# The first two gate tiles of each merge, loaded during the stage in front of it

## The reference

```
# first block, 3 branches of width 512          # second block, 5 branches of width 256
proj  = einsum('bsgc,gcd->bsgd', branches, w_branch[l])
gates = sigmoid(gate_logits.reshape(B, S, N_BRANCH, D_MODEL))     # gate_logits: columns of norm(x) @ w_in
x = x + sum(gates * proj, axis=2) @ w_out[l]
```

## Time and profile before

| | |
|---|---|
| median of three runs | 3766.71 us (3765.52, 3766.71, 5822.26) |
| profiled execution, its time | 3761.98 us |
| its span | 3760.2 us |
| mean granted TensorE clock | 0.961 |
| TensorE matmuls busy | 3514.6 us, 93% of the span |
| VectorE, ScalarE busy | 51%, 38% |
| HBM read, written | 307.09 MB, 38.80 MB |
| merges begin (first load issued) | 519.35, 1607.88, 2765.47, 3544.43 us |

### The profile page before, as it was taken

The page is one execution under the profiler, slowest core; times in us unless marked ns, Lnnn a source line. Parts: engine busy times, 40 slices in busy tenths (PEclk is TensorE's granted clock), DMA queues, the critical chain, the costliest instruction groups (busy, mean ns, idle before and its releaser), DMA issues. The chain is left out here.

```text
span 3760.2 us, 53758 instructions
## 1 busy us (share of the span) xinstructions
PE 3514.6 (93%) x21928; PEld 2747.8 (73%) x21928; DVE 1900.7 (51%) x3211; ACT 1419.0 (38%) x2319; POOL 61.4 (2%) x44
## 2 busy tenths in 40 slices
PE   8899789999999898989999999999989999899898
PEld 6678568788877786678788877756668778566586
DVE  6633433577557433434577353137655542367454
ACT  6222332344335221433344223255543333545532
POOL 0011000000000100000000000000000000000000
PEclk9999989999999998999999999999999999999999
DMA  4211323222332213142223233212133332122242
GB/s 151 67 59 33 139 107 109 79 99 97 107 124 76 60 55 112 48 146 101 84 95 107 83 125 112 91 41 87 49 132 134 111 110 85 37 90 65 99 140 76
DMA packets 101477, 350.04 MB, mean 93 GB/s; under 512 B 10945, under 2 KB 11329, under 8 KB 98433
## 3 DMA queue, kind: packets, MB, share of 16 engines
q1 hardware_dynamic: 101248, 346.85, 26.7%
HBM read 307.09 MB, written 38.80 MB: 92 GB/s over the span
## 5 line engine op out<-in xcount | busy, mean ns | idle before, releaser
L213 PE MATMUL bank<-h_high,weights_high 128*128 128x512 f32 x2464 | 1007.6, 409 | 69.6 <-DVE weights_low L1528 40.3
L214 PE MATMUL bank<-h_low,weights_high 128*128 128x512 f32 x2464 | 976.4, 396 | 0.0
L215 PE MATMUL bank<-h_high,weights_low 128*128 128x512 f32 x2464 | 975.3, 396 | 0.0
L213 PEld LDWEIGHTS bank<-h_high,weights_high 128*128 128x128 f32 x2464 | 471.6, 191 | 188.9 <-DVE weights_low L1528 42.8
L215 PEld LDWEIGHTS bank<-h_high,weights_low 128*128 128x128 f32 x2464 | 470.7, 191 | 104.0
L214 PEld LDWEIGHTS bank<-h_low,weights_high 128*128 128x128 f32 x2464 | 472.4, 192 | 100.4 <-issue 5.7
L1482 ACT CAST weights_high<-ring 128x1024 fp32r<-128x1024 f32 (+1 forms) x128 | 144.9, 1132 | 520.9 <-PE bank L215 467.5
L1528 DVE TENSOR_TENSOR weights_low<-ring,weights_high 128x1024 fp32r<-128x1024 f32 (+1 forms) x128 | 169.5, 1324 | 333.4 <-ACT weights_high L1482 333.2
L206 DVE TENSOR_TENSOR weights_low<-ring,weights_high 128x1024 fp32r<-128x1024 f32 x140 | 171.1, 1222 | 329.4 <-ACT weights_high L201 327.4
L201 ACT CAST weights_high<-ring 128x1024 fp32r<-128x1024 f32 x140 | 146.4, 1046 | 464.9 <-PE bank L215 458.0
L1655 ACT CAST weights_high<-ring 128x1024 fp32r<-128x1024 f32 (+1 forms) x116 | 132.6, 1143 | 337.9 <-PE bank L215 337.9
(11 more groups left out here) (431 smaller groups left out, 5252.2 us busy)
## 6 DMA issues: line engine op xcount, KB each, us to landing
ring<-in_in SPq DMA_DIRECT2D x136, 512.0 KB, 3.6
ring<-in_up SPq DMA_DIRECT2D x88, 512.0 KB, 3.2
x<-in_gates SPq DMA_DIRECT2D x64, 512.0 KB, 3.9
ring<-in_gates SPq DMA_DIRECT2D x64, 512.0 KB, 3.3
ring<-in_down SPq DMA_DIRECT2D x32, 704.0 KB, 4.1
ring<-in_out SPq DMA_DIRECT2D x32, 512.0 KB, 3.2
ring<-in_branch SPq DMA_DIRECT2D x16, 768.0 KB, 4.4
stored<-g_spill SPq DMA_DIRECT2D x16, 768.0 KB, 4.6
```

The lines of the kernel that those rows point to most:

```text
L213: pe.matmul(bank, core.wh[:, half, w], high, start=start, stop=False)
L214: pe.matmul(bank, core.wh[:, half, w], low, start=False, stop=False)
L215: return pe.matmul(bank, core.wl[:, half, w], high, start=False, stop=stop)
```

## The change

Every merge gets its tiles 0 and 1 from the stage in front of it. SP issues the two loads at the end of its program there, `branches` after the wait for the landed spills and a wait for the eight `y_mm` steps (the last readers of `scores` and `qdec`), `attention` after the wait for the spills alone. They go to the slots that the merge would use, columns 0 to 1023 and 1536 to 2559 in the first block, 0 to 1023 and 1280 to 2303 in the second. To keep those columns free, `vt` changes places with `scores` and `qdec`, `probsT` goes from columns 0 to 2047 to 3072 to 5119, and the two staging tiles go to 0 to 1023. A third set of four semaphores, made once, counts the landings; `merge` takes it as its `landed` and clears it at its end as it did its own. Sizes, number and order of the loads are the same, and so is all arithmetic.

```diff
+def load_merge(sp, core, n, slot_w, width, src):
+
+    sp.dma_start(core.ring[:, n * slot_w:n * slot_w + width], src).then_inc(core.landed[2][n], 16)
+
...
-def branches(nc, core, b, y_rw, y, y_sg, e):
+def branches(nc, core, b, y_rw, y, y_sg, e, first_gates):
...
             extra_transfers(sp, sems, core, e, begun=True)
+            sp.wait_ge(sems["y_mm"], 2 * NCH)
+            for n in range(2):
+                load_merge(sp, core, n, 12 * P, KD * P, first_gates(n))
...
                   "taken", "added", "y_rounded", "y_split", "m_rounded", "m_split", "projected", "x_added", *ROOT) as (block, sems):
+                  "taken", "added", "y_rounded", "y_split", "m_rounded", "m_split", "projected", "x_added", *ROOT,
+                  landed=core.landed[2]) as (block, sems):
...
-            for n in range(RING):
+            for n in range(2, RING):
                 load(n)
...
-            b["vt"] = core.ring[:, 0:4 * T].rearrange("p (c n) -> p c n", c=NCH)
-            b["scores"] = core.ring[:, 4 * T:8 * T].rearrange("p (c n) -> p c n", c=NCH)
-            b["qdec"] = core.ring[:, 8 * T:10 * T].rearrange("p (m t) -> p m t", m=2)
+            b["scores"] = core.ring[:, 0:4 * T].rearrange("p (c n) -> p c n", c=NCH)
+            b["qdec"] = core.ring[:, 4 * T:6 * T].rearrange("p (m t) -> p m t", m=2)
+            b["vt"] = core.ring[:, 6 * T:10 * T].rearrange("p (c n) -> p c n", c=NCH)
...
         @block.sync
         def _(sp):
             extra_transfers(sp, sems, core, e)
+            for n in range(2):
+                load_merge(sp, core, n, 2 * N_BR2 * P, KD * P, first_gates(n))
...
-                b["probsT"] = core.ring[:, 0:4 * T].rearrange("p (a h t) -> p a h t", a=2, h=2)
+                b["probsT"] = core.ring[:, 6 * T:10 * T].rearrange("p (a h t) -> p a h t", a=2, h=2)
...
-                    core.banks[7:8], [core.ring[:, n * T:(n + 1) * T] for n in (8, 9)]))
+                    core.banks[7:8], [core.ring[:, n * T:(n + 1) * T] for n in range(2)]), gates)
```

More of the change, by code:

```diff
@@ L1403, in merge @@
             phase(nc, *LANDED, "stored0", "stored1", "reloaded", "loaded", "gate_mm", "branch_mm", "rounded", "split", "gated", "opened",
-                  "taken", "added", "y_rounded", "y_split", "m_rounded", "m_split", "projected", "x_added", *ROOT) as (block, sems):
+                  "taken", "added", "y_rounded", "y_split", "m_rounded", "m_split", "projected", "x_added", *ROOT,
+                  landed=core.landed[2]) as (block, sems):
         def width(n):
@@ L1829, in block1_layer @@
                      *((("y", c), 4) for c in range(NCH)), ("sums", 8), ("turned", 8)],
-                    core.banks[6:7], [staging[:, n, :] for n in range(2)]))
+                    core.banks[6:7], [staging[:, n, :] for n in range(2)]), lambda n: w["gates1"][layer * (3 * KD) + n])
                 core.slots = core.ring
@@ L1835, in units @@
             return lambda n: w[name][layer * count + n]
-        one, other = core.landed
+        one, other = core.landed[0:2]
         with split_weights(nc, core, 12), nc.sbuf_tensor(f"y_high1{layer}", [P, 12, T], F32R) as y_high, \
@@ L2493, in _, with attention @@
                 beside(n)
-def attention(nc, core, b, pairs, forgotten, e):
+def attention(nc, core, b, pairs, forgotten, e, first_gates):
     banks, ident = core.banks, core.ident2
@@ L3075, in program @@
         core.count = 0
-        core.landed = [[stack.enter_context(nc.semaphore(f"{side}_{name}")) for name in LANDED] for side in ("one", "other")]
+        core.landed = [[stack.enter_context(nc.semaphore(f"{side}_{name}")) for name in LANDED] for side in ("one", "other", "third")]
         core.root, core.ones, core.eps, core.tiny = (buf(stack, "root", [T]), buf(stack, "ones", [P]), buf(stack, "eps", [2]),
```

## The result

The changed kernel takes 3746.7 us in the median of four runs (3745.53 to 3748.11). Of four runs of before one took 5822.26 us and is left out as a slow one; the others took 3765.52, 3766.71 and 3771.58 us. The ratio to them is 0.9943, with a 95% interval of 0.9929 to 0.9958. The forecast was 3751.8 us and 0.9960.

What follows compares the result with a forecast made beforehand. TensorE has work nearly throughout; its idle stretches at merge starts include waits for tile 0's load. Removing these gives 14.9 us, all else 0: 3766.7 - 14.9 = 3751.8 us; forecast 3744 to 3758, 8-of-10 range 3742 to 3761.

Steps and rivals of the forecast that it cites:

- The wait for tile 0: At each merge's start, SP's issue to ScalarE's cast: 15.29 us over four merges less 0.4, gain 14.9 (14.1 to 15.3).
- The wait for tile 1: At a merge's start, tile 1's load is covered by TensorE's work on tile 0: gain 0.
- SP's longer program, tenants, clearing: Two more loads in the stage in front, moved buffers, and four semaphores cleared at a merge's end: cost 0 each.
- The queue at a merge's start: Later loads issue 0.8 us earlier but are needed 3.3 to 4.9 us earlier; merge 3's stored gates are tight: cost 0.
- the guard of 2 us: In merge 3, TensorE keeps 2 us of room even if the stored gates come no earlier.
- Rival B: Gain given back within the merge by x's reload or the stored gates; if half were lost, 3759 us; chance 6%.
- The clock: Slow stretch after each merge's restart costs 1.4 to 2.9 us, left as is; scatter some +-3 us over four merges.
- rival A: Clock stays up after the shorter pause at each merge's start: some 8 us more gain, 3744 us; chance 8%.
- The range: Forecast case for the whole kernel: 3744 to 3758 us, at 77%.

Runs made afterwards that it cites:

- the tenants' run: Tenants change places and the third semaphore set is used, but all four first tiles load in the merge; against the kernel before: 3766.98 us, ratio 1.0000.
- tile 0 alone: The change with only tile 0 loaded ahead and tile 1 loaded first in the merge, against the kernel before: 3753.11 us, ratio 0.9962.
- The experiment with four loads more: Whole change plus four unread 512 KB loads behind the two ahead, awaited at the end of the stage in front; against the kernel before: 3750.75 us, ratio 0.9967.
- the first block's gain: Only the first block's two merges get tiles ahead, against the kernel before: 3757.34 us, ratio 0.9974.
- the halves: Whole change with tile 0's cast and subtraction in two halves of 512 columns, against the kernel before: 3747.60 us, ratio 0.9954.
- the fastest version: Whole change, tile 0's cast and subtraction in halves, and semaphore clearing shared by five engines, against the kernel before: 3718.37 us, ratio 0.9877.
- the second: The unaltered changed kernel timed in more rounds on one chip, against the kernel before: 3750.02 us, ratio 0.9955.
- the traffic added: Whole change plus four unread 512 KB loads, in all stages in front or in attention alone, against the kernel before: ratios 0.9967 and 0.9962.
- sharing the clearing: The kernel before with each stage's semaphores cleared by all five engines in turns instead of SP alone: 3742.20 us, ratio 0.9940.

## Why the prediction was right

*The wait for tile 0.* Read from the distance between SP's issue and ScalarE's cast, it was 15.29 us less 0.1 us per merge. ScalarE in fact starts 0.02, 0.02, 0.03 and 0.01 us after SP's first issue (the entries are 517.84, 1599.13, 2755.40 and 3533.13), so the term was 15.2, nearer its upper bound of 15.3 than the 14.9 forecast. TensorE's idle time fell by 4.75 us in merge 1 and 2.97 in merge 4, the sum of its waits by 15.0. Tenants and tile 0 alone show that nothing else carries the gain.

*The wait for tile 1.* Priced at nothing, and shown to within what can be measured: without that load ahead TensorE waits 0.4 us more in sum, and the time's interval includes the whole change's.

*SP's longer program, tenants, clearing.* Priced at nothing, and shown by the tenants' run and by SP's loads at 506.27, landing within 4.5 us. The experiment with four loads more shows what the cover is: there is room in `branches` for the two that the change lays there, and not for six when the stage has to wait for their landing.

*The queue at a merge's start.* The tight place was the stored gates of merge 3. They come 12.4 us after their issue at 2756.72, at 2769.1, and their sigmoid starts at 2769.55, right behind the gate's; the guard of 2 us wasn't needed. Rival B is out by the stage lengths and by the additivity of the first block's gain.

*The clock.* I gave it +-3 us. After the restart the granted clock stays at 0.50 for 4.7, 5.4, 6.2 and 3.3 us in the four merges; before it was 5.7, 3.8, 3.8 and 3.0, and in the changed kernel's second profile 4.5, 4.9, 3.5 and 3.1. That is scatter and no trend, and rival A (the clock stays up after a shorter pause) didn't happen in any of the four.

The reason that I gave against rival A was misread, though. The 0.69 ahead of merge 3 is a mean over a window in which the clock fell and rose again. Cut into pieces (us, TensorE's busy time and matmuls, granted clock, DMA share, GB/s), the kernel before shows the end of TensorE's work, the start of its pause, and the rest of the pause with the restart:

```profile
2761.30:2762.60 1.30, 1.27 (x24) 1.00 0.00 0
2762.60:2764.60 2.00, 0.00 (x0) 1.00 0.00 0
2764.70:2774.80 10.10, 3.71 (x9) 0.50 0.86 332
```

The clock is up when the pause begins and falls 2 us into it. In merges 2 and 4 of before it was also still at 1.00 some 4 us into the pause, and only ahead of merge 1 had it fallen with TensorE at work. So in three merges of four the low clock of the restart came with the pause and was not there before it, and a shorter pause may bear on it. Two cases speak for that. With the halves, merge 3 restarts after 4.3 us at 1.00, and the clock falls only 1.1 us later, for 3.4 us. In the fastest version the pause ahead of merge 3 is 3.7 us, and the clock stays up through it and through tile 0:

```profile
2739.20:2742.80 3.60, 0.00 (x0) 1.00 0.13 44
2742.85:2748.60 5.75, 5.75 (x25) 1.00 1.00 386
```

Its tile 0 takes 5.7 us, against 7.3 to 8.7 in the changed kernel. In the same profile merge 4 restarts at 0.50 after 3.6 us of pause, so a pause as short as this one promises nothing. That the changed kernel, with 5.3 to 7.4 us of idle time, saw nothing of rival A is as forecast; that nothing of the kind could come was argued from a mean, and the number came out right in spite of it.

The Trainium skill's rule for the price of a load ("DMA: Bandwidth & Descriptors", "Anatomy of one DMA") gives an estimate of 12.8 us for the four waits. Measured are 15.0. Most of the difference is merge 1's first load, with 4.9 us to land, and why that one is slow stays open. It was 4.7 us with tile 1 as the first load, and traffic issued right behind a load isn't enough for it: with four loads more behind them, the first loads ahead landed in 3.1 to 3.4 us.

*The range.* Its upper end doesn't follow from the terms that are named for it: 3766.7 less 14.1 and plus 3 us is 3755.6, and not 3758. Nothing hangs on it here.

*The size by time.* The first set of runs says 16 to 27 us, the second 12 to 22, the waits 15.0, the span 14.6. With the loads ahead the ratio is 0.9943 and 0.9955 for the changed kernel, 0.9962 with tile 0 alone, and 0.9967 and 0.9962 with the traffic added; all five have the same TensorE waits but for the fourth. I take 15 us to be its worth. That the first set's lower ratio is more than scatter isn't shown: the executions of one kernel differ with the clock that they are granted. Of the 23 of before that stand beside the whole change, the three that took 3774 us or more had a mean clock of 0.956 to 0.959, and the three below 3762 us had 0.961 to 0.962. The changed kernel's nine timed runs had 0.960 to 0.964. Whether a part of its gain is a higher clock can't be read from this, since an idle stretch taken out at the low clock raises the mean by itself.

## What to carry to other kernels

Where a stage begins with a load, compare the first consumer's start with the load's issue, not with its own idle time: ScalarE's two waits per merge had 53 us of idle to their name, and 15 were the transfer. Of the two tiles loaded ahead only the one that the first matmul needs counted here; the other lands beneath it. And once the load is gone, look at what stood beside it: sharing the clearing between two barriers was worth more over the program (22.6 us) than the loads ahead (some 15), with a diff of two lines. Last, a mean clock over a window should be cut into pieces before it is taken as the clock at the window's end.

## What the runs showed of the hardware

A semaphore clear costs an engine's queue unequal time: one every 0.06 us on SP, 0.10 on GpSimd, 0.12 on TensorE, so sharing it over five engines halves it (42.7 to 20.6 us) and doesn't divide it by five. The same stage scatters by microseconds between executions of one kernel, and in the stages looked at it goes with the granted clock: the first `attention` of the changed kernel took 236.1 us at a mean clock of 0.99 in one profile and 239.2 at 0.97 in another, and the stage ahead of the last `attention` took 89.8 us at 0.92 before and 93.6 at 0.87 after, with the same matmuls.

The granted clock fell within TensorE's pause, 2.1, 4.1 and 4.8 us after its last work, ahead of three merges of the kernel before, and stayed up through one pause of 3.7 us in the fastest version.
